# Feed-forward up projection: one product of 512 columns for both parts of the activation, and an addition on VectorE

## The reference, cut to what matters

```python
h2 = rmsnorm(x, norm_ffn_g)
up = causal_depthwise_conv(h2 @ w_up, conv_w, conv_b)   # 3 taps over the tokens
gate, val = jnp.split(up, 2, axis=-1)
return x + (jax.nn.silu(gate) * val) @ w_down
```

## Time and profile before

| | us |
|---|---|
| median of 3 runs | 1491.6 (1490.42 to 1492.27) |
| the profiled execution, its own time | 1492.93 |
| its span | 1491.1 |
| feed-forward stage in it, roughly | 217 to 421 |
| TensorE busy | 1419.8 |
| VectorE busy | 1043.9 |
| ScalarE busy | 824.2 |
| GpSimd busy | 190.4 |

### The profile page before, as it was taken

How to read it: one execution, slowest core, us unless ns; L and a number is a source line. 1 busy time by engine, 2 the same in 40 slices (tenths; PEclk the granted TensorE clock), 3 DMA queues, 4 the chain that set the end, 5 groups by cost and what they waited for, 6 DMA issues and landing times.

```text
span 1491.1 us, 30993 instructions
## 1 busy us (share of the span) xinstructions
PE 1419.8 (95%) x11674; PEld 1328.9 (89%) x11674; DVE 1043.9 (70%) x1848; ACT 824.2 (55%) x1548; POOL 190.4 (13%) x108
## 2 busy tenths in 40 slices
PE   5999899999979987889999999999999999999997
PEld 5989889999969987889999999999998888888885
DVE  5478657878767685569973978889985555555554
ACT  6344546656547773545444567777765545544553
POOL 0030000000000272047884000000000000000000
PEclk9999999999999997999999999999999999999999
DMA  6547556667734300354555554444446555555551
GB/s 238 191 153 256 186 198 212 241 229 267 253 102 139 100 4 4 114 183 157 185 183 189 179 168 138 138 139 141 142 143 218 191 195 193 191 194 196 189 192 56
DMA packets 68372, 253.00 MB, mean 170 GB/s; under 512 B 7584, under 2 KB 7840, under 8 KB 67488
## 3 DMA queue, kind: packets, MB, share of 16 engines
q1 hardware_dynamic: 67104, 245.40, 48.5%
q10 hardware_dynamic: 1152, 5.98, 1.0%
HBM read 249.25 MB, written 2.10 MB: 169 GB/s over the span
## 4 chain that ended last, share of the span: by engine, by line
PE 89%; DVE 5%; ACT 3%; issue 2%; POOL 1%; DMA 0%; ACTq 0%; DVEq 0%; POOLq 0%
PE bank L2105 23%; PE bank L1576 18%; PE bank L1577 18%; PE bank L1578 18%; PE bank L2071 4%; PE bank L1924 1%; DVE arena L947 1%; POOL arena L1565 1%; PE bank L2056 0%; DVE arena L944 0%; PE bank L1619 0%; PE bank L1634 0%; DVE w_lo L926 0%; DMA vec<-in_vec 0%; PE bank L1843 0%
## 5 line engine op out<-in xcount | busy, mean ns | idle before, releaser
L1576 PE MATMUL bank<-x_hi,w_hi 128*128 128x256 f32 x2120 | 620.2, 293 | 17.9 <-DVE x_lo L957 6.3
L926 DVE TENSOR_TENSOR w_lo<-raw,w_hi 128x1024 fp32r<-128x1024 f32 x364 | 445.2, 1224 | 228.8 <-ACT w_hi L497 225.9
L1578 PE MATMUL bank<-x_hi,w_lo 128*128 128x256 f32 x2120 | 604.5, 285 | 0.0
L1577 PE MATMUL bank<-x_lo,w_hi 128*128 128x256 f32 x2120 | 604.5, 285 | 0.0
L497 ACT ACTIVATE w_hi<-raw 128x1024 fp32r<-128x1024 f32 x416 | 439.0, 1056 | 182.7 <-PE bank L2105 167.2
L1576 PEld LDWEIGHTS bank<-x_hi,w_hi 128*128 128x128 f32 x2120 | 411.1, 194 | 28.3 <-issue 20.7
L1577 PEld LDWEIGHTS bank<-x_lo,w_hi 128*128 128x128 f32 x2120 | 412.1, 194 | 0.4
L1578 PEld LDWEIGHTS bank<-x_hi,w_lo 128*128 128x128 f32 x2120 | 411.1, 194 | 0.0
L2105 PE MATMUL bank<-w_hi,x_lo 128*128 128x512 f32 x508 | 156.5, 389 | 0.0
L2105 PE MATMUL bank<-w_lo,x_hi 128*128 128x512 f32 x508 | 156.4, 389 | 0.0
L2105 PE MATMUL bank<-w_hi,x_hi 128*128 128x512 f32 x508 | 156.3, 389 | 0.0
(11 more groups left out here) (316 smaller groups left out, 1488.1 us busy)
## 6 DMA issues: line engine op xcount, KB each, us to landing
raw<-in_u SPq DMA_DIRECT2D x128, 512.0 KB, 3.2
raw<-in_v SPq DMA_DIRECT2D x128, 512.0 KB, 4.3
raw<-in_w_in SPq DMA_DIRECT2D x54, 512.0 KB, 4.3
arena<-in_ada SPq DMA_DIRECT2D x48, 512.0 KB, 5.0
raw<-in_w_up SPq DMA_DIRECT2D x44, 512.0 KB, 4.9
raw<-in_w_down SPq DMA_DIRECT2D x22, 512.0 KB, 3.7
raw<-in_w_out SPq DMA_DIRECT2D x16, 512.0 KB, 4.3
raw<-in_w_q SPq DMA_DIRECT2D x16, 512.0 KB, 3.2
```

The source lines that it names most:

```text
L926: dve.tensor_tensor(w_lo[:, s], raw[:, s], w_hi[:, s].bitcast(F32), ALU.subtract).then_inc(lo_ready, 1)
L1576: pe.matmul(o, w, xh, start=start, stop=False, skip_group_check=True)
L1577: pe.matmul(o, w, xl, start=False, stop=False, skip_group_check=True)
L1578: return pe.matmul(o, wl, xh, start=False, stop=stop_, skip_group_check=True)
```

## The change

`x_hi` and `x_lo` become two halves of one tensor `x_pair`, so that for each k the high and the low part of the activation lie side by side. In the up projection (`reduce_pair`, and `reduce_pair_fresh` for the first tile) the high part of a weight tile meets both in one product of 512 columns that fills the whole bank: high x high on the left, high x low on the right. The low part of the weights meets the high part of the activation as before, in a product of 256 columns onto the left half. The two halves of the bank have yet to be added: ScalarE copies the right half to `up_right` in SBUF, VectorE adds it onto the left half in place, and ScalarE then goes on as before. `up_taken` and `conv_done` each count twice for a half where they counted once. The down projection and all other stages keep their three products.

```diff
-        x_hi = sb("x_hi", [P, KT, TOK], F32R)
-        x_lo = sb("x_lo", [P, KT, TOK], F32R)
+        x_pair = sb("x_pair", [P, KT, 2, TOK], F32R)
+        x_hi, x_lo = x_pair[:, :, 0], x_pair[:, :, 1]
...
+        up_right = qkv[:, 0:2]
...
                 for h in range(2):
                     split(b + h + AHEAD, i, 12)
                     act.wait_ge(chunk_used, b + h + 1 + 12 * i)
+                    act.activation(up_right[:, h], bank[h][:, TOK:2 * TOK], ACT.Copy).then_inc(S("up_taken"), 1)
+                    act.wait_ge(S("conv_done"), 4 * q + 2 * h + 1)
                     if q:
 
-                        act.wait_ge(S("conv_done"), 2 * (q - 1) + h + 1 + 8 * i)
+                        act.wait_ge(S("conv_done"), 4 * (q - 1) + 2 * h + 2)
...
-                act.wait_ge(S("conv_done"), 2 * q + 1 + 8 * i)
+                act.wait_ge(S("conv_done"), 4 * q + 2)
...
                 for h in range(2):
-                    dve.wait_ge(S("up_taken"), 2 * q + h + 1 + 8 * i)
+                    dve.wait_ge(S("up_taken"), 4 * q + 2 * h + 1)
+                    dve.tensor_tensor(bank[h][:, 0:TOK], bank[h][:, 0:TOK], up_right[:, h], ALU.add).then_inc(S("conv_done"), 1)
+                    dve.wait_ge(S("up_taken"), 4 * q + 2 * h + 2)
...
-                dve.wait_ge(S("conv_done"), 2 * q + 2 + 8 * i)
+                dve.wait_ge(S("conv_done"), 4 * q + 4)
...
+            def reduce_pair(b, o):
+
+                s = b % RING
+                pe.wait_ge(lo_ready, b + 1)
+                for k in range(KT):
+                    c = slice(k * P, k * P + P)
+                    pe.matmul(o[:, :], w_hi[:, s, c], x_pair[:, k].rearrange("p a t -> p (a t)"), start=k == 0, stop=False, skip_group_check=True)
+                    m = pe.matmul(o[:, 0:TOK], w_lo[:, s, c], x_hi[:, k], start=False, stop=k == KT - 1, skip_group_check=True)
+                m.then_inc(chunk_used, 1)
...
-            reduce_fresh(FFN, bank[0][:, 0:TOK], "norm_lo", KT)
-            reduce(FFN + 1, bank[1][:, 0:TOK])
+            reduce_pair_fresh(FFN, bank[0], "norm_lo", KT)
+            reduce_pair(FFN + 1, bank[1])
...
                 for h in range(2):
-                    pe.wait_ge(S("up_taken"), 2 * q - 1 + h + 8 * i)
-                    reduce(b + h, bank[h][:, 0:TOK], i, 12)
+                    pe.wait_ge(S("up_taken"), 4 * (q - 1) + 2 * h + 2)
+                    reduce_pair(b + h, bank[h])
```

More of the change, by code:

```diff
@@ L1641, in sum_summed, with reduce_pair_fresh @@
                 pe.matmul(bank[7][:, 0:TOK], ones, s_[:, 0], start=True, stop=True).then_inc(S("norm_ssq"), 1)
+            def reduce_pair_fresh(b, o, ready, before):
+                s = b % RING
+                pe.wait_ge(lo_ready, b + 1)
+                for k in range(KT):
+                    pe.wait_ge(S(ready), before + k + 1)
+                    c = slice(k * P, k * P + P)
+                    pe.matmul(o[:, :], w_hi[:, s, c], x_pair[:, k].rearrange("p a t -> p (a t)"), start=k == 0, stop=False, skip_group_check=True)
+                    m = pe.matmul(o[:, 0:TOK], w_lo[:, s, c], x_hi[:, k], start=False, stop=k == KT - 1, skip_group_check=True)
+                m.then_inc(chunk_used, 1)
             def reduce_fresh(b, o, ready, before=0):
```

## The result

The changed kernel takes 1519.44 us (median, 1518.66 to 1522.09) against 1490.82 us for the kernel before in the same sessions: the ratio is 1.0194, 95% interval 1.0181 to 1.0207. It is 28.6 us slower; the prediction was 27.8.

The account below looks back on a forecast made before the run. TensorE was taken to bound the kernel before, VectorE's chain after. Steps 0 to 20 + 26.6 us, a later first tap + 0.86 and the last step + 0.39 gave + 27.8: 1491.6 to 1519.4 us, range 1510 to 1533.

Parts of the forecast that it names:

- What bounds: Feed-forward stage: TensorE sets the pace before, with 1.03 us lead over VectorE in a step; VectorE's chain sets it after.
- The exchange: Each of 44 up tiles: VectorE's addition 0.42 us plus ScalarE's two instructions and hand-overs 0.90, together 1.32 us in VectorE's chain.
- The new step: Feed-forward step between first taps: 10.10 us with the long modulation sum, 9.90 without, where it was 8.64.
- The ends: Around the feed-forward steps: first tap 0.86 us later, step 21 + 0.39 us, TensorE's last tile only shifted.
- What TensorE gains: Up tiles: 13 ns for each of 352 products saved, 4.6 us in all; 2.78 us a tile instead of 2.88.
- rival 1: Feed-forward stage: TensorE keeps the pace and the exchanges are hidden, - 4.6 us, 1487 us; 4 in 100.
- TensorE's idle gaps: Each feed-forward step: TensorE idles 1.1 and 0.4 us.
- rival 3: Feed-forward steps: idle gaps make TensorE's clock fall, 1549 us, or 1634 at half clock throughout; 5 in 100.
- TensorE's waits before: Feed-forward stage of the kernel before: TensorE waits for VectorE once, 2.5 us at the last step.
- Rival 2: Feed-forward steps: only VectorE's work counts, its waits overlap, 8.45 us a step, about 1488 to 1492 us; 3 in 100.

Follow-up runs that it names:

- covered wait: Changed kernel with VectorE's low part of the next weight tile moved between the addition and the wait for `cv`: 1488.28 us, ratio to before 0.9982.
- products alone: Kernel before with only the up tiles' products changed to 512 and 256 columns; right half never added, no copy or addition: 1487.3 us, ratio 0.9975.
- grouped form: The products alone with a tile's eight 512 column products first, then its eight of 256, in 43 up tiles: 1488.41 us, ratio 0.9976.
- both grouped kernels: The products alone and both edits together, each with a tile's 512 column products first, then those of 256: 1488.41 and 1487.13 us.
- both edits together: Changed kernel with the covered wait's move, and VectorE writing the sum straight to `upad`, ScalarE's copy there dropped: 1486.94 us, ratio to before 0.9969.
- the control with the moved low part: Kernel before with only VectorE's low part of the weights moved ahead of the wait for `up_taken`: 1491.34 us, ratio to before 0.9995.

## Why the prediction was right, point by point

- **What bounds.** Right: TensorE before, VectorE's chain after. The step that carried it was to count VectorE's lead, 1.03 us, and not its busy share. The covered wait shows it from the other side.
- **The exchange.** 1.32 us was taken for each tile. Measured from the addition's start to the first tap's: 308.74 - 307.41 = 1.33. The addition took 0.42 to 0.43 us, the low one of the two forms that bounded it; writing to a bank costs nothing extra at this size.
- **The new step.** 10.10 with the sum, as measured. Without it 9.90 was said and 9.80 measured (245.06 to 254.86 between first taps): ScalarE's copy starts 0.95 us after the high part's start (252.17 to 253.12) and not 1.05. The 1.05 had been read where the copy still waited for TensorE: the tile's last product runs to 309.45 in that trace, and the copy starts at 309.49. 6 x 0.10 us. Against that, step 0 took 8.85 us and not 8.76, and two of the steps with the sum 10.19.
- **The ends.** The first tap comes at 226.42 and not 226.78. The last tile was taken as only shifted, with 0.8 us in the range for a longer idle time. TensorE now idles 6.0 us before it and does all 24 products at half clock, 0.213 us apart (from 443.80 to 448.50), where 15 were slow before: 0.9 us more.

```profile
445.00:448.00 3.00, 3.00 (x16) 3.00 (x15) 0.11 (x1) 0.36 (x2) 0.00 (x0) 0.50 0.74 249
```

- **The sum of these.** The last step's first tap is 26.8 us later instead of 27.4, and 0.4 + 0.9 more come behind it: 28.1, and 28.2 for the stage, which began 0.1 us earlier. The errors cancel: 27.8 for 28.2 is luckier than its parts.
- **What TensorE gains.** The term whose size was furthest off. 13 ns for a saved product and 4.6 us in all were said; the products alone won 2.7 us in the steps, since a pair takes 353 ns and not 347. It lay off the path and didn't matter to the time, but rival 1's 1487 rests on it; that the products alone measured 1487.3 doesn't bear it out, since in the profiled execution only 2.7 us came from the steps and 1.5 from the clock of the last tile, which is luck. What the Trainium skill gives for it (TensorE: Matmul & The Clock Gate, Part 1, "Wait — 56ns, not 53.3ns?"), 0.9 us by estimate, is about as far off to the other side; the measurement decides.
- **TensorE's idle gaps** were put at 1.1 and 0.4 us, counted from the pitch of the products, and are just that: 307.25 - 306.05 - 0.12 = 1.08 and 310.51 - 310.03 - 0.12 = 0.36. The profile's idle times, 0.92 to 0.96 and 0.20, are shorter because it gives the product before a length of 0.28 us, 0.16 more than its pitch.
- **The clock** (rival 3). 1.00 in the 20 us windows from 240 to 420 us with two gaps in each step, so gaps of 0.2 and 0.9 us didn't make it fall. The Trainium skill's rule on small idle times between groups of products (same page, "A second HAM failure mode: psum-queue depth-cycling") does not show in this trace at gaps of this size.
- **TensorE's waits before.** "Once" holds for the steps; the same view has one more wait of TensorE for VectorE at the stage's start (1.4 us for `x_lo`; 1.5 for `x_pair` in the changed kernel), so it changes nothing in the sum.
- **Rival 2**, that only the work counts, is refuted by the changed kernel and describes the covered wait: put the same instructions in another order and it comes true.

## What to carry to other kernels

Before work is added to an engine that "has room", take one period of its timeline and subtract from its idle time what ends on its own exchanges: only what ends on the bounding engine is room (here 1.03 us of 8.64 and not the window's 27%). An exchange of the form "A does something, B answers, A goes on" costs A the whole of B's answer unless A's own queue has work of that length to put in between; one moved line was worth 31 us here, over ten times the 2.7 us that the change itself could win. Once the wait was covered, making it shorter brought next to nothing (0.3 us in the stage).

## What the runs showed of the hardware that was not expected

- A product of 512 columns is 227 ns from the next where only such follow each other in the late stage, 231 within a group of eight in this one, and 236 when the two widths are in turn; there the one of 256 takes 117, where it takes 120 among its own kind. A pair in turn is 353. (Means of the starts from 240 to 400 us, in the products alone, 295 pairs, and their grouped form.)
- An idle time of 2.5 us of TensorE may or may not cost it the clock: the kernel before and both grouped kernels went on at half clock after it for the first 15 products, the products alone and both edits together at full clock. Its length alone doesn't tell either: the covered wait went on at full clock after 2.84 us, and the control with the moved low part fell to half from its third product on after 1.81 us (granted clock 0.50 from 414.30 to 417.50 us). That moves the stage by some 1.4 us from one profiled execution to another, half of what the new products win, and has to be taken out before two such kernels are compared by their traces.
